# One weight tile's low part on GpSimd: one subtraction over 1024 columns, or four over 256

## What is computed

```python
proj = u @ w_in[l]                                   # first block, in
h = h + jnp.concatenate([ya, yb], axis=-1) @ w_out[l]
z = h @ w_in                                         # second block, in
merged = (gates[:, :, 0] * (y_gla @ proj_gla) + gates[:, :, 1] * (y_ml @ proj_ml)
          + gates[:, :, 2] * (y_s5 @ proj_s5))
return merged @ w_out
...
gate, up = jnp.split(h @ w_in, 2, axis=-1)           # feed-forward
return (jax.nn.silu(gate) * up) @ w_out
```

## Time and profile before

| | |
|---|---|
| time, median of 3 runs | 2648.02 us (2646.36 to 2648.84) |
| the profiled execution | 2642.91 us |
| its span, first to last instruction | 2641.1 us |
| mean granted TensorE clock | 0.940 |
| TensorE busy | 2422.4 us (92%), 11312 matmuls |
| VectorE busy | 1071.2 us (41%) |
| GpSimd busy | 1104.2 us (42%), of which WL (L445) 662.4 us |
| DMA | 220.83 MB, mean 84 GB/s |

### The profile page before, as it was taken

How to read it: one execution, slowest core, us unless ns; L and a number is a source line. 1 busy time by engine, 2 the same in 40 slices (tenths; PEclk the granted TensorE clock), 3 DMA queues, 4 the chain that set the end, 5 groups by cost and what they waited for, 6 DMA issues and landing times.

```text
span 2641.1 us, 29887 instructions
## 1 busy us (share of the span) xinstructions
PE 2422.4 (92%) x11312; PEld 1939.4 (73%) x11312; DVE 1071.2 (41%) x1125; ACT 613.0 (23%) x668; POOL 1104.2 (42%) x1036
## 2 busy tenths in 40 slices
PE   4998887988699998999988999989889999999996
PEld 3777776767387876787766777877678888888875
DVE  6774544245521324143036633564673310233406
ACT  4543332132421222112011223222321100111111
POOL 3332222343131322222154413346566667666674
PEclk8999997999798998889788999999899999999998
DMA  3333333010211111101101113434243333333343
GB/s 137 115 108 104 103 103 112 24 56 24 102 45 44 41 48 41 64 24 56 40 26 47 42 50 108 145 126 135 65 143 95 97 102 103 101 98 95 104 152 119
DMA packets 64911, 220.83 MB, mean 84 GB/s; under 512 B 7344, under 2 KB 8512, under 8 KB 64832
## 3 DMA queue, kind: packets, MB, share of 16 engines
q1 hardware_dynamic: 61376, 207.14, 24.6%
q10 hardware_dynamic: 3456, 12.58, 1.2%
HBM read 194.53 MB, written 25.17 MB: 83 GB/s over the span
## 4 chain that ended last, share of the span: by engine, by line
PE 74%; DVE 9%; issue 5%; ACT 4%; DVEq 3%; DMA 2%; POOL 2%; ACTq 1%; POOLq 1%; SPq 0%
PE PG L725 27%; PE PG L522 16%; PE PG L569 13%; PE PG L960 5%; POOL WL L445 1%; PE PX L668 1%; PE PX L925 1%; DMA ADA<-ada_w 1%; PE PG L545 1%; PE PX L664 1%; DVE WK L1592 1%; DVE ADA L1601 1%; PE PX L592 1%; DMA WRAW<-hg_w 1%; PE PX L505 1%
## 5 line engine op out<-in xcount | busy, mean ns | idle before, releaser
L442 POOL TENSOR_TENSOR TOUCH<-TOUCH 128x2 f32<-128x2 f32 x282 | 86.9, 308 | 1441.1 <-PE PG L569 504.4
L445 POOL TENSOR_TENSOR WL<-WRAW,WH 128x1024 fp32r<-128x1024 f32 (+2 forms) x282 | 662.4, 2349 | 42.1 <-issue 3.4
L522 PE MATMUL PG<-UH,WH 128*128 128x512 f32 x832 | 329.6, 396 | 18.6 <-ACT WK L1296 8.0
L522 PE MATMUL PG<-UL,WH 128*128 128x512 f32 x832 | 327.0, 393 | 0.0
L522 PE MATMUL PG<-UH,WL 128*128 128x512 f32 x832 | 326.6, 393 | 0.0
L725 PE MATMUL PG<-UL,WH 128*128 128x512 f32 x800 | 312.6, 391 | 0.0
L443 POOL TENSOR_SCALAR WH<-WRAW 128x1024 fp32r<-128x1024 f32 (+2 forms) x282 | 299.8, 1063 | 0.0
L725 PE MATMUL PG<-UH,WH 128*128 128x512 f32 x688 | 268.5, 390 | 1.4 <-POOL WL L445 1.4
L725 PE MATMUL PG<-UH,WL 128*128 128x512 f32 x688 | 267.7, 389 | 0.0
L569 PE MATMUL PG<-UH,WH 128*128 128x512 f32 x544 | 240.6, 442 | 6.5 <-POOL WL L445 6.5
L569 PE MATMUL PG<-UL,WH 128*128 128x512 f32 x544 | 228.6, 420 | 0.0
(11 more groups left out here) (451 smaller groups left out, 3830.0 us busy)
## 6 DMA issues: line engine op xcount, KB each, us to landing
WRAW<-up_w SPq DMA_DIRECT2D x88, 512.0 KB, 3.5
ADA<-ada_w SPq DMA_DIRECT2D x48, 512.0 KB, 4.5
WRAW<-down_w SPq DMA_DIRECT2D x48, 512.0 KB, 3.6
WRAW<-out_w SPq DMA_DIRECT2D x24, 512.0 KB, 3.6
WRAW<-zg_w SPq DMA_DIRECT2D x24, 512.0 KB, 3.5
gates<-STG ACTq DMA_DIRECT2D x24, 512.0 KB, 2.6
WK<-gates SPq DMA_DIRECT2D x24, 512.0 KB, 3.3
H<-x SPq DMA_DIRECT2D x16, 512.0 KB, 5.6
```

Source lines behind the costliest of these rows:

```text
L442: pool.tensor_tensor(TOUCH[:, 0:2], TOUCH[:, 2:4], TOUCH[:, 4:6], ALU.add)
L445: pool.tensor_tensor(WL[:, r, 0:n], WRAW[:, r, 0:n], WH[:, r, 0:n].bitcast(F32), ALU.subtract).then_inc(w_split, 1)
L522: mm = pe.matmul(PG[:, 2 * s + half, :], w[:, r, P * k:P * k + P], x[:, k, tok], start=first and k == 0 and n == 0, stop=last and k == kbs ...
```

## The change

The subtraction that writes WL is issued in pieces of 256 columns. The semaphore is incremented by the last piece. Nothing else is changed; a tile of 256 columns still has one operation.

```diff
+LOW_PIECE = 256
 DVE_NORMS = (0, 1, 2, 4, 5)
 PE_NORMS = (3,)
...
                 pool.tensor_scalar(WH[:, r, 0:n], WRAW[:, r, 0:n], 1.0, 0.0, ALU.mult, ALU.add)
                 pool.drain()
-                pool.tensor_tensor(WL[:, r, 0:n], WRAW[:, r, 0:n], WH[:, r, 0:n].bitcast(F32),
-                                   ALU.subtract).then_inc(w_split, 1)
+                for at in range(0, n, LOW_PIECE):
+                    c = slice(at, at + LOW_PIECE)
+                    ins = pool.tensor_tensor(WL[:, r, c], WRAW[:, r, c], WH[:, r, c].bitcast(F32), ALU.subtract)
+                ins.then_inc(w_split, 1)
```

## The result

The changed kernel takes 2677.36 us (median of 4 runs, 2671.83 to 2682.93) beside 2648.43 for the kernel before on the same chip: **slower, ratio 1.0112 (95% interval 1.0096 to 1.0128)**. The forecast was +19.7 us and 2667, with 2684 as the upper end.

The account below looks back on a forecast made before the run. TensorE was taken as the bound (busy 92% of the span, matmuls 74% of the chain). Terms 11.1 + 8.6 + 5 - 5 = +19.7 us on the median 2648.0 gave 2667.7, say 2667; range 2652 to 2684.

Parts of the forecast that it names:

- TensorE's margins and the own length: Splits TensorE waits for and short down0/down1 tiles: 0.41 us more per full tile, 6.3 + 4.8, 11.1 us in all.
- The down stages: down0 and down1: short tiles of 18 matmuls leave TensorE no margin; 12 x (0.41 - 0.01) = 4.8 us.
- An operation over 512 columns costs GpSimd 0.45 us: Between two GpSimd operations: one VectorE operation gets in, 1.02 - 0.57 = 0.45 us; 0.9 taken for 1024 columns.
- VectorE between the pieces: VectorE operations entering between pieces delay GpSimd: 8.6 us at exposed splits plus 5 us at thin margins.
- exposed split: Splits TensorE waits for: one VectorE operation inserted at each, 7 x 0.9 plus 5 x 0.45, 8.6 us.
- two thin places: Start of up0 and the stretch 1890 to 1930 us: insertions exceed TensorE's small margin, 2.5 us each, 5 us.
- What VectorE gets back: VectorE's chain operations behind WL: a quarter of about 21 us of waiting is won, -5 us (ends 0 and -15).
- rival 2: Norms and residuals: short holds end VectorE's serial steps earlier and its gain wins; -7 us, 2641; chance 6%.
- The first: At the piece boundaries: GpSimd keeps the port, VectorE waits as before, only 11.1 us are paid; 2659; chance 16%.
- The third: At all splits: pieces cost next to nothing, VectorE's gain and loss cancel; 0 to 4 us, 2650; chance 9%.
- The signs set for the profile: Expected in the trace: down0 loads about 0.4 us late, shorter L1695 and L2196, 27 to 35 WL waits near 60 us.

Follow-up runs that it names:

- the run with the memset: Against the kernel before: WL stays one operation, a GpSimd memset of 416 columns (96 in a 512-column tile) precedes WH; 2658.65 us, ratio 1.0031.

## Why the prediction was right in sign and low in size

1. **TensorE's margins and the own length: right.** 2.81 us for four pieces, 0.41 for a tile. It was priced at 11.1 us; the run with the memset measured 8.2 (4 to 12). The down stages were put at 4.8 us of it and, with their other waits and the operations there, at about 8 together; alone they measured 8.2. What was wrong is "in the other stages a tile has 48 matmuls and margins of several us": in out2b the first weight loads of tiles 141, 142 and 145 came 0.44, 0.23 and 0.89 us behind the end of the split. (Both waits on half tiles are in glu, tiles 103 and 104, and none in proj; the sum is the same.)
2. **"An operation over 512 columns costs GpSimd 0.45 us": right,** 0.44 to 0.46 in all kernels looked at, even ahead of a piece of 64 columns. For 1024 columns I took 0.9, the trace has 0.97. The up loops fit (0.86 against 1.10), and TensorE's difference is flat there.
3. **"VectorE between the pieces", 13.6 us: the step that came out low.** The price of a turn was right and the count was wrong. I counted one insertion for each exposed split (7 over 1024 columns, 5 over 512) and one to three at two thin places. The trace has one at every boundary as long as VectorE has work queued, and in the first block it has: L1682 five in a row, L1738 and L1740 in turn. There the low part gets 6.5 us long, 2.7 us more than with one insertion (2.81 + 0.97), and in the second block the splits of tiles 141, 142, 145 and 152, with 0.2 to 0.9 us to spare, become exposed. By my terms the first block was worth some 7 us (5 x 0.9 and the own length at its waits); it measured 14.6 (11 to 18) with the 3 us gain of rg_w inside. That difference, 8 to 10 us, is as large as the gap between +19.7 and +29. It is not insertions into WL alone: at tile 25 WH takes a turn too (0.98 us), and part of it is the longer matmuls. The two thin places were put at 2.5 us each; in the trace tiles 144 to 153 lose 8.3 us and tiles 155 to 160 lose 4.1, against which the norms give back what item 4 says. That the sum came within 10 us of the result is partly luck: losses and gains left out of it offset one another.
4. **"What VectorE gets back", -5 us: of the right order, by the reason given.** Of 143 us less waiting, the kernels with pieces in some stages show about 3 us from the first row of scans and 1 to 6 at the norms of out2b. In the changed kernel itself TensorE is 3.6 us ahead at tile 8, and at the two rows of norms it has 8.2 and 8.7 us back, right behind stretches in which it had lost 6.7 and 8.3 at splits. Where the rest of the waiting went was not traced. At the first row of norms rival 2 had the mechanism right (with four stages in pieces the wait for L2165 goes from 14.4 to 6.8 us), and in those kernels it pays more than the splits of out2b cost.
5. **Rivals.** The first fell to the alternation. The third (pieces cost nothing) fell to 2.81 and 3.39 us. The signs set for the profile came out: first loads in down0 late by 0.4 us, L1695 below 2 us, L2196 near 1200 (1013), 27 to 35 waits (36); their sum was put near 60 us and is 76.8, which fits the same miscount.

The Trainium skill ("SBUF — State Buffer", Who interferes with whom) says that whoever issues first holds the shared port for the whole instruction. The rows bear that out for one instruction; what decided here is that the holder doesn't keep it for its next instruction when the other engine is waiting, as the 1.15 and 1.66 us from start to start show where undisturbed pieces have 0.69.

## What to carry to other kernels

Cutting an operation on GpSimd in pieces puts a door into it at every cut, and VectorE goes through each one as long as it has a queue: price a split as own length (0.14 us a cut) plus, at each cut, one turn of the other engine (here 0.45 us for an operation of 0.69, and 0.97 for one of 1.21), and take the count from the length of its queue, not from the one operation that is waiting now. Cut only where VectorE's row is what TensorE waits for next and that wait shrinks by more than the later splits cost: at the norms of out2b it did (7.6 us against 5.5), in the first block from tile 8 on it did not. So it is decided stage by stage: four stages out of 25 in pieces were worth -9.8 us, all of them +29 to +34.

## What was not expected of the hardware

- Two engines with queued work on the port take turns one instruction at a time, for all the lengths seen here: pieces of 256 columns (0.69 us from start to start) wait for operations of 1.2 us each time, and at tile 53 for one of 2.32 us (2.48 from start to start). The other engine need not gain by it: the seven L1679 around tile 25 took 10.16 us beside long splits and 11.06 beside pieces.
- The price of a turn doesn't depend on the size of the piece behind it: 0.46 us ahead of 256 columns, 0.45 ahead of 128, 0.44 ahead of 64 and ahead of all 1024, for the same operation over 512 columns.
- A GpSimd subtraction has about 0.14 us of its own beside 2.2 ns for a column: 2.40 us for one piece of 1024 columns, 2.54 for two, 2.81 for four, 3.39 for eight.
